# Opening of a decoder layer: first weights in two transfers along their depth, first norm's weight row spread by TensorE, second token tile turned after the first tile's projection

## The reference

```python
h = rms_norm(x, norm1_g)                   # x * rsqrt(mean(x*x) + 1e-6) * norm1_g
qa, ka, va, qb, kb, vb, gb, gate_a, gate_b = split(h @ w_in)
qa = rope(rms_norm(qa, q_norm_g), positions)     # 4 heads, two 64-wide halves each
ka = rope(rms_norm(ka, k_norm_g), positions)     # angles = positions * freq, cos and sin of them
lam = exp(sum(lambda_q1*lambda_k1)) - exp(sum(lambda_q2*lambda_k2)) + lam_init
oa = rms_norm(diff_attention(qa, ka, va, lam), diff_subln_g)
ob = group_norm(retention(rope(qb), rope(kb), vb))
x = x + (sigmoid(gate_a) * (oa @ w_branch_a) + sigmoid(gate_b) * ((silu(gb) * ob) @ w_branch_b)) @ w_out
x = x + hier_moe(rms_norm(x, norm2_g))     # 32 experts, top-1 of 4 groups, then top-2 of 8
```

## Time and profile before

| | |
|---|---|
| median of 3 runs | 1473.28 us (1472.91 to 1475.1) |
| the profiled execution's own time | 1475.07 us |
| its span, first to last instruction | 1473.2 us |
| TensorE busy | 1422.8 us, 97% of the span |
| VectorE, ScalarE, GpSimd busy | 999.5, 828.7, 403.1 us |
| mean granted TensorE clock | 0.987 of full speed |

### The profile page before, as it was taken

How to read it: one execution, slowest core, us unless ns; L and a number is a source line. 1 busy time by engine, 2 the same in 40 slices (tenths; PEclk the granted TensorE clock), 3 DMA queues, 4 the chain that set the end, 5 groups by cost and what they waited for, 6 DMA issues and landing times.

```text
span 1473.2 us, 19518 instructions
## 1 busy us (share of the span) xinstructions
PE 1422.8 (97%) x7296; PEld 1199.7 (81%) x7297; DVE 999.5 (68%) x1444; ACT 828.7 (56%) x1342; POOL 403.1 (27%) x462
## 2 busy tenths in 40 slices
PE   4899999999999999999999969999999999999996
PEld 4788988988988788888888858888888888888885
DVE  6754664664664433344332557999999999999996
ACT  5553453453353322223233236888888888888883
POOL 2224424434424300000000110233333333333331
PEclk9999999999999999999999979999999999999999
DMA  6110210210210333363340549999999999999992
GB/s 213 32 44 1 62 44 1 62 44 2 62 44 1 84 89 86 95 181 87 86 179 12 218 154 393 380 377 390 390 381 385 389 389 393 394 393 395 385 381 84
DMA packets 134032, 286.39 MB, mean 194 GB/s; under 512 B 18864, under 2 KB 97840, under 8 KB 109360
## 3 DMA queue, kind: packets, MB, share of 16 engines
q1 hardware_dynamic: 119216, 263.79, 49.6%
q0 software_dynamic: 13248, 21.00, 3.9%
q10 hardware_dynamic: 1472, 0.32, 0.1%
HBM read 287.16 MB, written 25.17 MB: 212 GB/s over the span
## 4 chain that ended last, share of the span: by engine, by line
PE 88%; DMA 4%; DVE 2%; ACT 1%; issue 1%; POOL 0%; POOLq 0%; DVEq 0%; ACTq 0%
PE proj L105 17%; PE proj L107 17%; PE proj L106 17%; PE scores L107 6%; PE scores L105 6%; PE scores L106 6%; DMA w_slot<-in_w_up 4%; PE outs L764 2%; PE scores L694 2%; PE scores L572 1%; PE turned L105 1%; PE turned L107 1%; PE turned L106 1%; DVE w_low L1750 1%; PE outs L855 1%
## 5 line engine op out<-in xcount | busy, mean ns | idle before, releaser
L1750 DVE TENSOR_TENSOR w_low<-w_slot,w_high 128x2048 fp32r<-128x2048 f32 x192 | 430.7, 2282 | 0.1
L1190 ACT ACTIVATE w_high<-w_slot 128x2048 fp32r<-128x2048 f32 x190 | 353.4, 1911 | 23.9 <-DMA w_slot<-in_w_up 9.9
L105 PE MATMUL proj<-w_high,xeH 128*128 128x512 f32 x512 | 204.3, 399 | 4.4 <-DVE xeL L1853 1.9
L107 PE MATMUL proj<-w_high,xeL 128*128 128x512 f32 x512 | 201.0, 393 | 0.0
L106 PE MATMUL proj<-w_low,xeH 128*128 128x512 f32 x512 | 200.4, 391 | 0.0
L1380 POOL DMA_INDIRECT out<-y,ids_rows x31 | 86.5, 2791 | 344.0 <-DVE y L1863 344.0
L1003 ACT ACTIVATE wCH<-wC_in 128x1024 fp32r<-128x1024 f32 x48 | 47.6, 1052 | 154.9 <-DMA wC_in<-in_w_branch_b 154.9
L1444 DVE TENSOR_TENSOR wCL<-wC_in,wCH 128x1024 fp32r<-128x1024 f32 x48 | 56.7, 1232 | 91.5 <-ACT wCH L1003 91.5
L105 PEld LDWEIGHTS proj<-w_high,xeH 128*128 128x128 f32 x512 | 97.1, 190 | 26.6 <-issue 3.9
L107 PEld LDWEIGHTS proj<-w_high,xeL 128*128 128x128 f32 x512 | 96.7, 189 | 21.0
L106 PEld LDWEIGHTS proj<-w_low,xeH 128*128 128x128 f32 x512 | 97.0, 189 | 19.3
(11 more groups left out here) (299 smaller groups left out, 3154.9 us busy)
## 6 DMA issues: line engine op xcount, KB each, us to landing
w_slot<-in_w_gate SPq DMA_DIRECT2D x64, 1024.0 KB, 11.5
w_slot<-in_w_up SPq DMA_DIRECT2D x64, 1024.0 KB, 11.7
w_slot<-in_w_down SPq DMA_DIRECT2D x64, 1024.0 KB, 12.3
wC_in<-in_w_in SPq DMA_DIRECT2D x32, 512.0 KB, 4.9
wB_in<-in_w_in SPq DMA_DIRECT2D x16, 512.0 KB, 6.4
wA_in<-in_w_in SPq DMA_DIRECT2D x12, 512.0 KB, 5.8
x_all<-in_x SPq DMA_DIRECT2D x4, 1024.0 KB, 8.8
wC_in<-in_w_branch_a SPq DMA_DIRECT2D x16, 256.0 KB, 5.6
```

The lines of the kernel that those rows point to most:

```text
L105: pe.matmul(out, lh, rh, start=start, stop=False)
L107: return pe.matmul(out, ll, rh, start=False, stop=stop)
L1190: act.activation(w_high[slot][:], w_in6[slot][:], ACT.Copy).then_inc(S["w_split"], 1)
L1750: dve.tensor_tensor(w_low[slot][:], w_in6[slot][:], w_high[slot][:].bitcast(F32), ALU.subtract).then_inc(S["w_lows"], 1)
```

## The change

It touches the first 35 us, and two later places of the first head. SP starts with its transfers and signals the free buffers afterwards; the constants go through SP instead of ScalarE's queue. Of x only tile 0 is loaded ahead of the weights, tile 1 behind them, under a semaphore of its own. The weights come as six transfers, slices 0 to 3 and then 4 to 7. The norm's weight row is loaded once into one partition, and TensorE multiplies it by a column of ones into two PSUM banks, which ScalarE copies to `g1_row`. The positions come as 8 rows of 128 and are transposed by TensorE. Tile 0 goes through its whole projection before tile 1 is turned; tile 1's remainder stands behind tile 0's rotation on VectorE. ScalarE loads the sine table first and the exponential table after the weights, with a one-element activation each. The making of `lam` moves into step 1. `norm_tile(7)` moves ahead of a weight split.

```diff
+            sp.dma_start(consts[:], T["consts"][:, 0:LATE]).then_inc(S["consts_in"], DMA)
+            sp.dma_start(x_all[:, 0, :], x_v[:, 0, :]).then_inc(S["x_in0"], DMA)
+            sp.dma_start(g1_one[:], T["norm1_g"][0:1]).then_inc(S["g1_in"], DMA)
+            for half, done in enumerate(("wA_first", "wA_landed")):
+                for j, col in enumerate((QA, KA, VA)):
+                    sp.dma_start(wA_in[:, 4 * half:4 * half + 4, 128 * j:128 * j + 128],
+                                 w_in_v[:, 4 * half:4 * half + 4, col:col + 128]).then_inc(S[done], DMA)
+            sp.dma_start(x_all[:, 1, :], x_v[:, 1, :]).then_inc(S["x_next"], DMA)
             for name in STARTS_FREE:
                 sp.sem_inc(S[name], FREE)
-            sp.dma_start(x_all[:, 0:2, :], x_v[:, 0:2, :]).then_inc(S["x_in0"], DMA)
-            sp.dma_start(g1_row[:], T["norm1_g"][0].partition_broadcast(P)).then_inc(S["g1_in"], DMA)
...
-            load_A(0)
...
+            pe.wait_ge(S["ang_step"], 1)
+            pe.transpose(TB[:, 0:8], pos_rows_f[:], ident[0:8, 0:8]).then_inc(S["first_turned"], 1)
+            pe.wait_ge(S["g1_in"], DMA + 1)
+            for half, spare in enumerate((PROJ[1], OB)):
+                pe.matmul(spare[:, :], ones_row[:], g1_one[:, half * 512:half * 512 + 512], start=True, stop=True
+                          ).then_inc(S["first_turned"], 1)
             turn_tile(0)
-            turn_tile(1)
...
                     project(s, [6, 7])
+                    if h == 0 and s == 0:
+                        turn_tile(1)
...
             angle(dve.tensor_scalar(turns[:], turns[:], -MAGIC, None, ALU.add))
-            for part in TWO_PI:
+            for n, part in enumerate(TWO_PI):
                 angle(dve.scalar_tensor_tensor(ang[:], turns[:], -part, ang[:], ALU.mult, ALU.add))
+                if n == 0:
+                    mean_tile(0)
+                if n == 1:
+                    norm_tile(0)
...
-            for i in range(2):
-                mean_tile(i)
-            for i in range(2):
-                norm_tile(i)
             low_tile(0)
             for k in range(8):
                 low(wAL[:, k, :], wA_in[:, k, :], wAH[:, k, :], S["wA_high"], k + 1, S["wA_low"])
-            low_tile(1)
-            mean_tile(2)
-            norm_tile(2)
-            head_steps(0, FILL[:1])
...
+            mean_tile(1)
+            norm_tile(1)
+            head_steps(0, FILL)
```

And inside a step, on VectorE:

```diff
+                    if h == 0 and s == 0:
+                        low_tile(1)
+                        mean_tile(2)
                     if h == 0 and s < 5:
                         mean_tile(s + 3)
+                    if h == 0 and s == 0:
+                        norm_tile(2)
                     if h == 0 and s == 4:
                         low_tile(6)
+                        norm_tile(7)
```

More of the change, by code:

```diff
@@ L154, in decoder_layer @@
         x_ms = small[:, 32:40]
-        posf = small[:, 40:48]
         g2x = small[:, 48:56]
-        posi = sb("posi", [P, 8], I32)
         R_HT, R_A, R_B, R_OT = place(64 * KIB), place(24 * KIB), place(32 * KIB), place(32 * KIB)
@@ L174, in decoder_layer @@
         oTL = sb("oTL", [P, 8, 1024], F32R, at=R_OT)
+        pos_rows = sb("pos_rows", [N_TILES, P], I32, at=R_B + 2 * KIB)
+        pos_rows_f = sb("pos_rows_f", [N_TILES, P], F32, at=R_B + 3 * KIB)
+        g1_one = sb("g1_one", [1, 1024], F32, at=R_B + 20 * KIB)
+        ones_row = sb("ones_row", [1, P], F32, at=R_B + 24 * KIB)
         lam_rows = sb("lam_rows", [P, 4, 64], F32, at=R_B + 4 * KIB)
@@ L1090, in head_steps @@
                                            accum_out=rowsum[:, c:c + 1]).then_inc(S["exped"], 1)
-            act.dma_start(consts[:], T["consts"][:, 0:LATE]).then_inc(S["consts_in"], DMA)
-            act.dma_start(posi[:], T["positions"][0].rearrange("(i p) -> p i", p=P),
-                          allow_slow_non_contiguous=True).then_inc(S["pos_in"], DMA)
+                    if h == 0 and s == 1:
+                        act.wait_ge(S["lam_step"], 2)
+                        act.activation(lam_e, lam_s, ACT.Exp).then_inc(S["lam_step"], 1)
+            act.dma_start(pos_rows[:], T["positions"][0].rearrange("(i p) -> i p", p=P)).then_inc(S["pos_in"], DMA)
             for j, n in enumerate(("q_norm_g", "k_norm_g")):
@@ L1276, in _ @@
             pool.tensor_copy(causalB[:], const("causal")).then_inc(S["tables_made"], 1)
-            x_powers(range(2))
-            pool.wait_ge(S["trig_done"], 2)
+            x_powers(range(1))
+            pool.wait_ge(S["trig_done"], 3)
             pool.wait_ge(S["gains_in"], 2 * DMA)
@@ L1474, in head_steps @@
                         low_tile(s + 1 if s < 5 else 7)
+                    if h == 0 and s == 1:
+                        lam_sums()
                     if u2 == "A":
@@ L1564, in head_steps @@
                         split_weights(s)
+                    if h == 0 and s == 1:
+                        lam_finish()
                     if u1 == "A":
@@ L1572, in head_steps @@
                                                  ).then_inc(S["sums_used"], 1)
-                    if h == 0 and s < 5:
+                    if h == 0 and s < 4:
                         norm_tile(s + 3)
```

63 lines of the change are left out of this document (35 added, 28 removed).

## The result

| | before | changed |
|---|---|---|
| median | 1472.23 us (22 runs, 1469.87 to 1475.67) | 1474.81 us (22 runs, 1472.36 to 1477.69) |
| ratio to before, 95% interval | | 1.0018 (1.0012 to 1.0023) |
| its profiled execution | 1475.07 us, span 1473.2 | 1474.15 us, span 1472.2 |

The predicted 1472.3 us is missed by 2.5 us. The two profiled executions say the opposite of the medians, since that of before was an unusually late one.

A forecast was written before the change was run, and what follows sets the result against it. TensorE, busy 97% of the span, was taken as the bound, with time only in its waits and low clock. From 1475.07 us, −0.8 (tile 2's projection), −1.25 (`norm_tile(7)`) and −0.75 (clock) gave 1472.3 us; range 1469.6 to 1475.4.

The forecast's parts named there:

- the sum: From 1475.07: 0.8 off for tile 2's projection, 1.25 for tile 7's normalisation, 0.75 for the clock, giving 1472.3 us.
- Two f32 matmuls of 512 columns ... 1.8 for both.: Opening: TensorE spreads the norm's weight row at 0.9 us per product, so the first normalisation starts at 9.2.
- the named way to lose: Slower rival: tile 0 and the norm's row land up to 10.0, not 6.5, giving 1476.5 us; chance 0.08.
- the 4.2 us to be gained here: Opening: the first normalisation was to start at 9.2 instead of 13.43, 4.2 us earlier.
- `norm_tile(1)` waits for GpSimd ... Here the gain is handed back.: Opening: tile 1's normalisation waits for GpSimd's tables until 20.6; its projection starts at 25.6, 1.5 us later than before.
- A low stretch follows here too, but one as short: Low clock after the stall before tile 1's projection costs 1.9 us against 2.65 before: 0.75 us gained.
- a full one: Clock's bad bound: low clock through all of tile 1's projection and turn, 3.0 us lost, 0.35 more than before.
- `norm_tile(7)` ... 1.25 us.: Tile 7's normalisation starts at 62.44, not 63.67, taking 1.25 us from TensorE's 1.8 us of standing still.
- `lam` out of the way: With ScalarE free, `qkTH` starts at 30.15 and tile 2's projection at 32.5, 0.8 us earlier than before.
- Against the profiled execution's own 1475.07.: Base of the terms: the profiled execution, the slowest of three shown, its excess about what its low stretch cost.
- The rest waits on TensorE and is shifted whole.: All gains lie ahead of 70 us; everything behind keeps its length and only moves in time.
- the rule weighed in the prediction: ScalarE table switch costs 2.66 us with drain; it would hold `qkG` until about 22.1, some 0.4 us more.

The follow-up runs named there:

- before, again: A second profiled execution of the unchanged kernel, 1472.31 us, near the median and used as the base for comparing profiles.
- e4: Changed kernel with tile 1 loaded ahead of the weights and turned and projected right behind tile 0, ahead of the rotation: 1468.34 us, 0.9971 of before.
- the repeat: The changed kernel timed once more, unedited, as control of the experiments: 1475.05 us, 1.0019 of before.
- e8: Changed kernel with `lam` back between step 0 and step 1 and tile 7's normalisation late, as before: 1476.70 us, 1.0031 of before.
- e2: Kernel before with only `lam` made inside step 1 and the exponential table loaded where `lam` stood: 1468.20 us, 0.9975 of before.
- e14: Changed kernel with the reduce of the counts made twice on VectorE ahead of the 2048-column subtraction: 1474.24 us, 1.0007 of before.
- e15: Kernel before with three one-column memsets at the very start of VectorE's program: 1472.88 us, 0.9997 of before.
- e6: Changed kernel with tile 1 again ahead of the rotation and the norm's weight row spread by a transfer: 1470.32 us, 0.9986 of before.
- e3: Changed kernel with 24 unread 384-column matmuls, 11 ahead of the turn of tile 1 and 13 behind: 1472.89 us, 1.0004 of before.
- e16: Kernel before with the subtraction of piece 2 placed ahead of the copy, reduce and cast of the counts: 1474.34 us, 1.0005 of before.
- e10: Kernel before with `lam` in step 1, tile 7's normalisation early and the change's early transfers, positions still in 4-byte packets: 1472.23 us, 1.0001 of before.

## Why the prediction was wrong, by its steps

By the sum, turn 3 was to stand at 37.7, the middle to take 832.6 and the last part 600.2. The profiled execution of the changed kernel has 40.33 (2.7 more), 830.7 (1.9 less) and 601.2 (1.0 more), and the median is 0.7 above that execution. Two steps failed above all: the price of the two products that spread the norm's row, which the rest of the opening carried on, and the sentence that all behind 70 us is only shifted. The low stretch near 500 us, whose absence the sum didn't foresee, hid 1.7 us of this; that the time stayed inside the range is luck to this extent.

**"Two f32 matmuls of 512 columns ... 1.8 for both."** The mis-sized term of the first chain: 1.9 us each, with the copies behind them 1.7 apart. The pace by columns was right (0.94 us a matmul, forecast 0.9), but the trace records each of the two products as two matmuls, where a turned piece is one. `norm_tile(0)` stood at 11.02, not 9.2. Tile 0's landing (6.3 against 6.5), its turn and the splits took about what was forecast, and all of it stood 1.8 to 2.2 late (`wAL` done at 21.2, not 19.0). The landing of the transfers, the named way to lose, came as forecast. Even the 4.2 us to be gained here were mostly the lateness of one execution: in "before, again" the first normalisation starts at 11.46, not 13.43.

**"`norm_tile(1)` waits for GpSimd ... Here the gain is handed back."** Right in mechanism: released by GpSimd at 23.09 (forecast 20.6), tile 1's projection released by `hTL` at 27.88 (25.6): the 1.8 us from above and 0.7 more, since the tables took 5.4 us (17.11 to 22.52) and not 4.46. More of them lay beside VectorE's weight split (before 18.65 to 22.86, changed 17.46 to 21.19), and there they take longer. Two of these table instructions before, without and with the split beside them, and two of the changed kernel, with and without:

```profile
17.73 0.32 POOL L1292 TENSOR_TENSOR gain_sin<-sin_t,gains 128x64 f32<-128x64 f32 x1
...
18.88 0.62 POOL L1292 TENSOR_TENSOR gain_sin<-sin_t,rope_sin 128x64 f32<-128x64 f32 x1
```

```profile
20.15 0.63 POOL L1311 TENSOR_TENSOR gain_sin<-sin_t,gains 128x64 f32<-128x64 f32 x1
...
21.93 0.32 POOL L1311 TENSOR_TENSOR gain_sin<-sin_t,rope_sin 128x64 f32<-128x64 f32 x1
```

Tile 1's projection is 3.8 us later than the 24.11 of before, and e4 shows this order to be the main loss of the opening.

**"A low stretch follows here too, but one as short"** (3.4 us). It is twice that, 6.8 us here and in the repeat (26.1 to 32.9), but begins while TensorE still waits. What it costs is 2.4 us in tile 1's projection (5.6 us for 3.25), against 1.9 in the sum and 3.0 for the bound of "a full one": the length was wrong, the price only by 0.5. With 2.3 us from the start of tile 1, this makes the 4.6 us by which tile 2's projection was later (37.12, forecast 32.5). Tile 2 itself then ran at 2.4 GHz, in 3.2 us and not 5.9, so the turn of tile 3 is at 40.33 against 37.7 by the sum: 2.7 us, of which 2.3 are the late start of tile 1 and 0.5 the clock.

**"`norm_tile(7)` ... 1.25 us."** Right: TensorE's wait is 0.46 us, 1.8 before. **"`lam` out of the way"**: `qkTH` at 34.78 no longer waits for the exponential, which comes at 38.89, but by e8 it wouldn't have waited for it in this order either, tile 1's projection being so late. The gain counted for it isn't there. As the only edit of the kernel before (e2) it gives 4 us, mostly by the clock.

**"Against the profiled execution's own 1475.07."** That execution is 2.8 us above the median of 22. A forecast of 2.8 us down from it was a forecast of no change without saying so. Its lateness was not the low clock alone, as supposed: its first turn also stood at 14.86 rather than 12.89, and its weights were split from 18.10 rather than 16.32 on.

**"The rest waits on TensorE and is shifted whole."** It isn't. A wait 840 us behind the change grew from 5.6 to 7.8 us, because the start of VectorE's subtraction moved by 0.25 us, from behind that of GpSimd's gather to ahead of it; over all profiled executions this goes with 1.9 us. Without it, by e14, the changed kernel stands at 1.0007 (0.9998 to 1.0016): not told from before, since the 3.7 us lost in the opening are nearly met by the 1.3 us at tile 7 and the missing low stretch near 500 us. Why that stretch is absent isn't tested. None of the ten profiled executions built on the changed kernel has it, but of the ten built on the kernel before only six do.

What stays open: why the idle of 0.28 us in VectorE's program stands where it does (e15 shows that the instructions ahead move it, not by what rule), what makes the low stretch near 500 us come and go, and e6.

## What to carry to other kernels

When an edit of an opening moves the time by a few tenths of a per cent, compare the stretches behind it too, on marks that both kernels share: some 1.9 of the 2.6 us came from a wait 840 us behind the opening. Take the base of a sum from several executions, not from the profiled one. When an instruction has no row of its own, ask how many records one call of it leaves in a trace before scaling its price from another. And before a tile's turn is moved behind a projection, follow what the new wait on TensorE brings: here 2 x 2.3 us of standing still cost another 2.4 us at the lower clock, and harmless extra matmuls in their place (e3) took that back.

## What the runs showed of the hardware

A long VectorE instruction holds GpSimd's gather: 3.34 us where the subtraction of 2048 columns starts 0.12 or 0.13 us ahead (seven profiled executions, all of the changed order), 3.04 where it starts 0.44 ahead (e16), 1.31 or 1.32 where it starts 0.13 us or more behind it (ten) and where it starts 0.02 ahead (e4 and e6, where the subtraction took 2.34 and not 2.28). The Trainium skill, "Trainium Architecture — The Big Picture", section "What this means for kernel authors", says that VectorE and GpSimd share a pair of ports under an exclusive lock; the trace agrees, for the gather ends 1.2 us behind the subtraction in both held cases.

GpSimd's table instruction of 64 columns (`gain_sin`) takes 0.31 or 0.32 us, and 0.62 to 0.64 beside VectorE's weight split, in both kernels. No experiment took the split away from beside it.

A transfer of 1024 packets of 4 bytes landed 2.8 us after its issue in the kernel before and 9.2 us where another queue's packets of 4 KB were issued ahead of it (e10). An f32 product with one row and 512 columns took 1.9 us in two matmuls, at the pace of 1.2 GHz: the 384-column matmuls from 16.30 on start 0.32 us apart, as in the stretch from 26.3 to 33.1, though the trace has no record of the clock before 19.4 and the windows view gives 1.00. ScalarE's table load at 20.56 took 1.28 us, and the next activation began 0.01 us behind it. By the rule weighed in the prediction (the Trainium skill, "ScalarE: Activation LUTs", section "What ACT_TABLE_LOAD costs", 1.38 us of drain beside the load) it would have held `qkG` until about 23.4, as an estimate; `qkG` began at 22.20, 0.15 us behind TensorE. The trace disagrees with the rule.
